# Two query tiles of one grouped head weighed by high and low values side by side, instead of two heads of one query tile

## The chip, the cores and the metric

One core of a Trainium2 chip runs the whole program. The metric is the device time of one execution in microseconds, the median of three runs. Engine names are those of the profile: PE is TensorE's matrix multiplication and PEld its loading of stationary operands, DVE is VectorE, ACT is ScalarE, POOL is GpSimd, SP issues the DMAs.

## The reference, cut to what matters

A backbone of two layers works on 512 latent tokens behind 256 context tokens, width 1024. Each layer projects the normalised input, attends in two ways (grouped heads and differential heads) beside a convolution, merges the three branches with gates, and ends in a SwiGLU feed-forward part. The grouped heads are the ones that the change touches: 8 query heads of width 64 share 2 key and value heads.

```python
def gqa_attend(q, k, v):
    s = jnp.einsum('bqkgd,btkd->bkgqt', q * ATTN_SCALE, k).astype(jnp.float32)
    p = jax.nn.softmax(s, axis=-1).astype(v.dtype)
    return jnp.einsum('bkgqt,btkd->bqkgd', p, v)
...
        o_gqa = blocked_queries(lambda qb: gqa_attend(qb, gk_all, gv_all), gq)
...
        if not last:
            oc_gqa = gqa_attend(gqc, gkc, gvc)
```

Latent queries see all 768 keys, context queries only the 256 context keys, and those are computed in layer 0 alone.

## The kernel before

Every float32 product is made of three matmuls on operands split into a high part and a low rest: high by high, high by low, low by high (`product`, lines 670 to 672).

**Heads and items.** The attention part of a layer is a walk over "heads" j = 0 to 7. Heads 0 to 3 are pairs of grouped query heads, one for each key and value head: the two members are called maps, m = 0 and m = 1, and sit in rows 0 to 63 and 64 to 127. Heads 4 to 7 are differential. An item g is one head j and one tile of 128 queries: six tiles (i = 0 to 5) in layer 0, the last two of them context queries with 256 keys (k0 = 4), and four (i = 0 to 3) in layer 1. For each item PE computes the scores of both maps (`scores`, into the PSUM tensors sco0 and sco1), DVE takes the row maximum (L1678) and ACT the exponential (L1118, M<-sco), DVE divides by the sum (`gqa_probs`, L1697 and L1698), PE transposes the probabilities into an aux bank (`turn_probs`, L874), ACT copies out the high part (`turned_hi`) and DVE the low part (`turned_lo`), and PE weighs the values with them (`weigh`). Scores run one item ahead.

**Weighing before.** The stationary operand holds the values of both maps, 64 columns each, and the moving operand the 128 queries of map 0 beside the 128 queries of map 1. Of the product only the diagonal blocks (values of map m with queries of map m) are used, and `grouped_out` copies these two out, 64x128 each. An item takes 6 x 3 matmuls of 256 columns, a context item 2 x 3.

**Slots.** Two slots per item hold projections of the next head: `slot(j, s)` runs a number of chunks, given by the tables FILL and SECOND, each chunk three matmuls (384 columns wide in layer 0, 512 in layer 1). In layer 1 a grouped head before the last has 3, 3, 2, 2, 2, 2, 1, 1 chunks in its eight slots, the first eight of them for the next query projection q, the rest for a convolution input a. When q is finished (slot 2, which is the first slot of item i = 1), ACT evacuates it in two passes and splits a weight tile (WHI, L1114); in slot 3 PE sums its squares (`head_sums`, L839), ACT makes the root, DVE rotates it (`rope`), in slot 4 DVE scales it, and in slot 5 ACT and DVE split it. `scores` of the next head waits for that split (semaphore qk).

**Order and banks.** Each engine takes its instructions in written order. Heads 0 to 2 are `late`: the item before is weighed in the middle of the next item, between its second transposition and its second slot; head 3 weighs at the item's end. PE has two acc banks (weighing and chunks) and two aux banks (transpositions and sums); an aux bank that holds turned probabilities comes free when `turned_lo` has read it on DVE.

Of the kernel before, what the change touches and what calls it, by code (L numbers as in the profile page):

```python
# [192 lines left out]
def build(nc, xT, vecs, consts, wdw, w_mod, w_in, w_gate, w_br, w_out, w_fi, w_fo, out):  # L193
    x_next = nc.dram_tensor("x_next", (P, KC, LAT), F32).ap()

    with ExitStack() as ctx:
# [14 lines left out]
        with nc.sbuf_tensor("UNDER", [P, 2 * KC * TOK], F32), nc.sbuf_tensor("SOONB", [P, 2 * KC * TOK], F32) as SOONB:  # L211
# [5 lines left out]
        STG = sb("STG", [P, STAGES, KC * P], F32)  # L217
        X = sb("X", [P, KC, TOK], F32)
# [32 lines left out]
               [v4(RB, o * TOK, 6, 256) for o in (6, 10)]]  # L251

        BR = RB[:, :].rearrange("p (s k t) -> p s k t", s=2, k=KC)
# [59 lines left out]
        late = lambda j: j < 3  # L313
        pt = lambda j, g: PTS[g % 2 if late(j) else 0]
# [311 lines left out]
        def _(pe):  # L626
# [251 lines left out]
            def weigh(name, j, g, k0, turned):  # L878
# [4 lines left out]
                for k in range(k0, 6):  # L883
                    mm = product(dst[:, 0:256], VB[:, kv, 0, k, :], VB[:, kv, 1, k, :],
                                 pt(j, g)[0][:, k, :], pt(j, g)[1][:, k, :], k == k0, k == 5)
                at[name] = c.at("acc")
                close_acc(mm, acc.index(dst))
# [6 lines left out]
            def attention(l):  # L894
# [28 lines left out]
                for g, (j, i, q, k0) in enumerate(items):  # L923
# [5 lines left out]
                    turn_probs((l, g, 0), 2 * (g % 2), k0)  # L929
                    slot(j, 2 * i)  # L930
# [6 lines left out]
                    if g and late(items[g - 1][0]):  # L937
                        k1 = items[g - 1][3]
                        weigh((l, g - 1, "o"), items[g - 1][0], g - 1, k1,
                              [at[(l, g - 1, m), p] for m in range(2) for p in range(parts(k1))])  # L940
                    if j < 4 and not late(j):
                        slot(j, 2 * i + 1)
                        weigh((l, g, "o"), j, g, k0, [at[(l, g, m), p] for m in range(2) for p in range(parts(k0))])
                        continue
# [137 lines left out]
        def _(act):  # L1082
# [83 lines left out]
            def values_hi(name, kv):  # L1166
                for i in range(2):
                    b = take_aux(at[name, i])
                    fn(VB[:, kv, 0, 3 * i:3 * i + 3, :], v4(aux[b], 0, 3, P), ACT.Copy, sem="vhi")
# [449 lines left out]
        def _(dve):  # L1619
# [143 lines left out]
            def attention(l):  # L1763
# [28 lines left out]
                for g, (j, i, q, k0) in enumerate(items):  # L1792
# [6 lines left out]
                    if j < 4:  # L1799
                        slot(j + 1, 2 * i)  # L1800
# [486 lines left out]
```

## Time and profile before

| | |
|---|---|
| median of 3 runs | 2417.32 us (2414.1 to 2419.98) |
| span of the profiled execution | 2417.6 us |
| PE busy, of the span | 2347.1 us, 97% |
| PEld busy | 2117.3 us, 88% |
| DVE busy | 1379.6 us, 57% |
| ACT busy | 1027.8 us, 43% |
| grouped heads of layer 0 (scores of head 0 to those of head 4) | about 88 to 267 us |
| grouped heads of layer 1 | about 1484 to 1647 us |

No time of the profiled execution is given beside its span. Busy time of PE counts matmuls that overlap each other, so the distance from one start to the next tells what a matmul costs.

### The profile page before, as it was taken

How to read it: one execution, taken by the hardware profiler on the slowest of the kernel's cores; microseconds unless marked ns; L12 is line 12 of the kernel's file. 1: busy time of each engine (PE TensorE's matmuls, PEld its weight loads, DVE VectorE, ACT ScalarE, POOL GpSimd, SP SyncE). 2: the span in 40 equal slices, each digit the busy share in tenths (PEclk: the TensorE clock that was granted, in tenths of full speed). 3: DMA queues.
4: the chain of work that ended last, by engine and by line, in shares of the span. 5: the costliest groups of instructions: out<-in, count | busy, mean ns of one | idle time of the engine just before them, and what ended most of it. 6: DMA issues, size and time to landing. Idle time of an engine off the chain costs nothing.

```text
span 2417.6 us, 33460 instructions
## 1 busy us (share of the span) xinstructions
PE 2347.1 (97%) x13144; PEld 2117.3 (88%) x13144; DVE 1379.6 (57%) x2097; ACT 1027.8 (43%) x2039; POOL 698.9 (29%) x513
## 2 busy tenths in 40 slices
PE   7999999999999989999999999999999998999999
PEld 3888999999999989999999997777878887888887
DVE  5666777689967735553343347667888944211111
ACT  4666676642253242212212237666764354422222
POOL 2211112100034424343343333112220154444443
PEclk9999999999999989999999999999999999999999
DMA  6100111022124413433443421011113323333333
GB/s 255 45 19 27 40 40 36 31 92 88 61 83 137 164 57 114 132 109 116 129 134 98 127 96 53 27 36 45 50 35 92 100 89 125 92 100 96 97 96 96
DMA packets 134667, 208.99 MB, mean 86 GB/s; under 512 B 12528, under 2 KB 66032, under 8 KB 134384
## 3 DMA queue, kind: packets, MB, share of 16 engines
q1 hardware_dynamic: 134512, 206.86, 27.1%
q8 instruction: 105, 1.72, 0.3%
q14 instruction: 50, 0.41, 0.1%
HBM read 202.62 MB, written 4.19 MB: 86 GB/s over the span
## 4 chain that ended last, share of the span: by engine, by line
PE 77%; DVE 14%; ACT 6%; issue 3%; DMA 1%; SPq 0%; DVEq 0%; ACTq 0%
PE acc L670 20%; PE acc L672 20%; PE acc L671 20%; DVE X L1758 4%; PE aux L670 3%; PE aux L671 3%; PE aux L672 3%; DVE RB L1635 2%; PE sco L861 2%; PE aux L874 2%; ACT M L1118 2%; DVE M L1635 1%; DVE NM L1678 1%; ACT WHI L1114 1%; DVE WLO L1635 1%
## 5 line engine op out<-in xcount | busy, mean ns | idle before, releaser
L586 POOL TENSOR_TENSOR WLO<-STG,WHI 128x512 fp32r<-128x512 f32 (+2 forms) x500 | 692.0, 1406 | 1700.9 <-ACT WHI L1114 1536.2
L670 PE MATMUL acc<-H,WHI 128*128 128x384 f32 (+2 forms) x1976 | 712.8, 361 | 14.5 <-DVE H L1911 8.7
L671 PE MATMUL acc<-H,WHI 128*128 128x384 f32 (+2 forms) x1976 | 696.9, 353 | 0.0
L672 PE MATMUL acc<-H,WLO 128*128 128x384 f32 (+2 forms) x1976 | 696.7, 353 | 0.0
L1114 ACT ACTIVATE WHI<-STG 128x512 fp32r<-128x512 f32 (+2 forms) x616 | 330.2, 584 | 402.1 <-PE acc L672 365.4
L670 PEld LDWEIGHTS acc<-H,WHI 128*128 128x128 f32 x1976 | 375.4, 190 | 44.4 <-issue 13.0
L672 PEld LDWEIGHTS acc<-H,WLO 128*128 128x128 f32 x1976 | 375.0, 190 | 25.4
L671 PEld LDWEIGHTS acc<-H,WHI 128*128 128x128 f32 x1976 | 375.8, 190 | 24.0
L670 PE MATMUL acc<-RB,WHI 128*128 128x384 f32 (+1 forms) x816 | 288.5, 354 | 3.2 <-DVE RB L1635 1.5
L1635 DVE TENSOR_TENSOR T<-G,acc 128x384 f32<-128x384 f32 (+1 forms) x101 | 60.2, 596 | 405.4 <-PE acc L672 290.1
L672 PE MATMUL acc<-RB,WLO 128*128 128x384 f32 (+1 forms) x816 | 287.6, 352 | 0.0
L671 PE MATMUL acc<-RB,WHI 128*128 128x384 f32 (+1 forms) x816 | 287.6, 352 | 0.0
L1758 DVE SCALAR_TENSOR_TENSOR X<-U,WDW,X 128x783 f32<-128x783 f32 (+1 forms) x248 | 219.3, 935 | 4.9 <-ACT X L1118 3.3
L1976 DVE SCALAR_TENSOR_TENSOR X<-acc,MOD,X 128x384 f32<-128x384 f32 (+3 forms) x124 | 65.0, 547 | 242.9 <-PE acc L672 242.8
L670 PE MATMUL aux<-H,WHI 128*128 128x384 f32 (+1 forms) x552 | 197.6, 358 | 1.0 <-DVE WLO L1635 1.0
L671 PE MATMUL aux<-H,WHI 128*128 128x384 f32 (+1 forms) x552 | 195.8, 355 | 0.0
L672 PE MATMUL aux<-H,WLO 128*128 128x384 f32 (+1 forms) x552 | 195.6, 354 | 0.0
L1678 DVE TENSOR_REDUCE NM<-sco 128x1 f32<-128x768 f32 (+1 forms) x160 | 134.8, 844 | 66.0 <-PE sco L861 65.9
L670 PEld LDWEIGHTS acc<-RB,WHI 128*128 128x128 f32 x816 | 153.2, 188 | 15.3 <-DVE RB L1635 1.8
L671 PEld LDWEIGHTS acc<-RB,WHI 128*128 128x128 f32 x816 | 153.2, 188 | 10.7
L672 PEld LDWEIGHTS acc<-RB,WLO 128*128 128x128 f32 x816 | 153.2, 188 | 10.6
L1118 ACT ACTIVATE M<-sco,NM 128x768 f32<-128x768 f32 (+1 forms) x160 | 131.1, 820 | 61.4 <-DVE NM L1678 61.2
(148 smaller groups left out, 2934.3 us busy)
## 6 DMA issues: line engine op xcount, KB each, us to landing
STG<-in_w_fi SPq DMA_DIRECT2D x176, 256.0 KB, 2.7
M<-in_w_mod SPq DMA_DIRECT2D x56, 512.0 KB, 4.9
STG<-in_w_in SPq DMA_DIRECT2D x104, 256.0 KB, 2.7
STG<-in_w_gate SPq DMA_DIRECT2D x96, 256.0 KB, 2.7
STG<-in_w_fo SPq DMA_DIRECT2D x64, 256.0 KB, 2.7
STG<-in_w_br SPq DMA_DIRECT2D x96, 128.0 KB, 2.1
FIRST<-in_w_mod SPq DMA_DIRECT2D x8, 1024.0 KB, 20.2
SOONB<-in_w_mod SPq DMA_DIRECT2D x16, 512.0 KB, 4.1
```

Of the source, the lines that this page charges most:

```text
L586: nc.gpsimd.tensor_tensor(WLO[:, s, a:a + w], STG[:, g, a:a + w], WHI[:, s, a:a + w].bitcast(F32), ALU.subtract).then_inc(S("w_split"), 1)
L670: nc.tensor.matmul(dst, lh, rh, start=first, stop=False)
L671: nc.tensor.matmul(dst, lh, rl, start=False, stop=False)
L672: return nc.tensor.matmul(dst, ll, rh, start=False, stop=last)
L861: mm = nc.tensor.matmul(sco[m][:, o:o + w], QB[h, j % 2, x, q:q + P], KB[h, kv, y, a:a + w], start=n == 0, stop=n == 2)
L874: t = nc.tensor.transpose(dst[:, n * P:(n + 1) * P], PR[:, slot, (k - k0) * P:(k - k0 + 1) * P], IDENT)
L1114: nc.scalar.activation(WHI[:, s, a:a + w], STG[:, g, a:a + w], ACT.Copy).then_inc(S("w_hi"), 1)
L1118: ins = nc.scalar.activation(dst, src, f, **kw)
L1635: return nc.vector.tensor_tensor(dst, a, b, op)
L1678: nc.vector.tensor_reduce(NM[:, slot:slot + 1], sco[m][:, 0:n], AX_X, ALU.max, negate=True).then_inc(S(f"max{m}"), 1)
L1758: nc.vector.scalar_tensor_tensor(o, like(l, U[:, ch * UW + t:ch * UW + t + w0]), WDW[:, l, ch, t:t + 1], o, ALU.mult, ALU.add).then_inc(S( ...
L1976: nc.vector.scalar_tensor_tensor(X[:, j, s:s + m], src[:, s - a:s - a + m], MOD[:, l, part, j, st:st + 1], X[:, j, s:s + m], ALU.mult, ALU ...
```

## The change

Weighing is done once for two query tiles (items i = 0 and 1, 2 and 3, 4 and 5) and one map at a time. The stationary operand is now the high values of one map beside its low values, 64 columns each (`VGM`, two matmuls a key tile: one with the high probabilities moving, one with the low), and the moving operand has 256 columns, the queries of both tiles. Rows of the high values and of the low values come out apart, so ACT copies one half (`grouped_lo`) and DVE adds the other to it (`grouped_sum`), which also frees the acc bank. Map 0 is weighed at the end of the odd item, map 1 in the next item, after its first transposition and ahead of its first slot. Turned probabilities of map 1 lie in a new tensor XP, in the upper half of the room of X. The exception of head 3 is gone, so that DVE turns the low part of map 1 behind `gqa_probs` for all grouped heads. Two bias copies of the convolution in layer 1 move from head 3 to head 4.

```diff
+        with nc.sbuf_tensor("UNDERX", [P, 4 * TOK], F32), nc.sbuf_tensor("XP", [P, 2 * 6 * 256], F32R) as XP:
+            pass
...
+        VG = RB[:, 8 * TOK:10 * TOK].rearrange("p (k b d) -> p k b d", k=6, b=4)
+        VGH, VGL = VG[:, :, 0:4:3, :], VG[:, :, 1:3, :]
+        VGM = RB[:, 8 * TOK:10 * TOK].rearrange("p (k m c) -> p k m c", k=6, m=2)
...
-        late = lambda j: j < 3
-        pt = lambda j, g: PTS[g % 2 if late(j) else 0]
+        grouped_pair = lambda item: item[0] < 4 and item[1] % 2
...
+            def weigh_map(l, g, k0, m):
+                wait_free("aux", *(at[(l, e, m), p] for e in (g - 1, g) for p in range(2 if k0 == 0 else 1)))
+                dst = open_acc()
+                for k in range(k0, 6):
+                    for s in range(2):
+                        mm = nc.tensor.matmul(dst[:, 0:256], VGM[:, k, m, :], PTS[m][s][:, k, :],
+                                              start=(k == k0 and s == 0), stop=(k == 5 and s == 1))
+                at[l, g, "o", m] = c.at("acc")
+                close_acc(mm, acc.index(dst))
...
                     turn_probs((l, g, 0), 2 * (g % 2), k0)
+                    if g and grouped_pair(items[g - 1]):
+                        weigh_map(l, g - 1, items[g - 1][3], 1)
                     slot(j, 2 * i)
...
-                    if g and late(items[g - 1][0]):
-                        k1 = items[g - 1][3]
-                        weigh((l, g - 1, "o"), items[g - 1][0], g - 1, k1,
-                              [at[(l, g - 1, m), p] for m in range(2) for p in range(parts(k1))])
...
                     slot(j, 2 * i + 1)
+                    if grouped_pair((j, i)):
+                        weigh_map(l, g, k0, 0)
...
-            def grouped_out(l, g, j, q):
-                b = take(at[l, g, "o"])
-                for m in range(2):
-                    rows = slice(m * HEAD, m * HEAD + HEAD)
-                    fn(X[rows, j, q:q + P], acc[b][rows, m * P:(m + 1) * P], ACT.Copy,
-                       sem=f"acc_free{b}" if m else "oraw")
+            def grouped_lo(l, g, j, q, m):
+                b = take(at[l, g, "o", m])
+                rows, lows = (slice(n * HEAD, n * HEAD + HEAD) for n in (m, 1 - m))
+                fn(X[rows, j, q - P:q + P], acc[b][lows, 0:256], ACT.Copy, sem="glo")
...
                     if after:
                         exp(0, g + 1, after[3])
                         exp(1, g + 1, after[3])
+                    if g and grouped_pair(items[g - 1]):
+                        grouped_lo(l, g - 1, items[g - 1][0], items[g - 1][2], 1)
                     slot(j + 1, 2 * i)
...
+            def grouped_sum(l, g, j, q, m):
+                b, _ = banks["acc"][at[l, g, "o", m]]
+                c.step("glo")
+                dve.wait_ge(S("glo"), c.at("glo"))
+                rows = slice(m * HEAD, m * HEAD + HEAD)
+                o = X[rows, j, q - P:q + P]
+                tt(o, o, acc[b][rows, 0:256], ALU.add).then_inc(S(f"acc_free{b}"), 1)
...
                         maximum(1, g + 1, after[3])
+                    if g and grouped_pair(items[g - 1]):
+                        grouped_sum(l, g - 1, items[g - 1][0], items[g - 1][2], 1)
                     if j < 4:
                         slot(j + 1, 2 * i)
-                    if j < 4 and not late(j):
-                        turned_lo((l, g, 1), pt(j, g), P, k0)
                     if after and after[0] < 4:
                         gqa_probs(g + 1, after[3])
...
                     slot(j + 1, 2 * i + 1)
+                    if grouped_pair((j, i)):
+                        grouped_sum(l, g, j, q, 0)
```

Where the instructions stand is read from the program's order. On PE, at the end of item i = 1 of a grouped head in layer 1, before: the last matmuls of the item before being weighed (acc<-RB), the two chunks of slot 3 (acc<-H), the sums of squares for the next query projection (aux<-M,K), and the next scores.

```order
L671 MATMUL acc<-RB 128x256
L672 MATMUL acc<-RB 128x256
L670 MATMUL acc<-H,WHI 128x512
L671 MATMUL acc<-H,WHI 128x512
L672 MATMUL acc<-H,WLO 128x512
L670 MATMUL acc<-H,WHI 128x512
L671 MATMUL acc<-H,WHI 128x512
L672 MATMUL acc<-H,WLO 128x512
L839 MATMUL aux<-M,K 128x256 x2
L861 MATMUL sco<-RB 128x512 x6
```

The same place of PE after the change, from the second transposition of the item (aux<-K,M) on; L903 is `weigh_map`.

```order
L881 MATMUL aux<-K,M 128x128 x6
L677 MATMUL acc<-H,WHI 128x512
L678 MATMUL acc<-H,WHI 128x512
L679 MATMUL acc<-H,WLO 128x512
L677 MATMUL acc<-H,WHI 128x512
L678 MATMUL acc<-H,WHI 128x512
L679 MATMUL acc<-H,WLO 128x512
L846 MATMUL aux<-M,K 128x256 x2
L903 MATMUL acc<-RB 128x256 x12
L868 MATMUL sco<-RB 128x512 x6
```

Between the second transposition and the sums of squares there stand two chunks now and no weighing; map 0 is weighed behind the sums.

On DVE, item i = 2 of such a head before: maximum of map 0, low part of the turned map 0, maximum of map 1, scaling of q (M<-M,R), division of both maps, low part of the turned map 1, low part of q.

```order
L1678 TENSOR_REDUCE NM<-sco 128x1
L1635 TENSOR_TENSOR RB<-aux,RB 128x3x128 x2
L1678 TENSOR_REDUCE NM<-sco 128x1
L1635 TENSOR_TENSOR M<-M,R 128x512
L1697 RECIPROCAL RL<-L 128x1
L1698 TENSOR_SCALAR M<-M,RL 128x768
L1697 RECIPROCAL RL<-L 128x1
L1698 TENSOR_SCALAR M<-M,RL 128x768
L1635 TENSOR_TENSOR RB<-aux,RB 128x3x128 x2
L1635 TENSOR_TENSOR RB<-M,RB 128x512
```

The same item of DVE after the change, with the sum of map 0 of the pair before ahead of it.

```order
L1652 TENSOR_TENSOR X<-X,acc 64x256
L1698 TENSOR_REDUCE NM<-sco 128x1
L1652 TENSOR_TENSOR RB<-aux,RB 128x3x128 x2
L1698 TENSOR_REDUCE NM<-sco 128x1
L1652 TENSOR_TENSOR X<-X,acc 64x256
L1652 TENSOR_TENSOR M<-M,R 128x512
L1726 RECIPROCAL RL<-L 128x1
L1727 TENSOR_SCALAR M<-M,RL 128x768
L1726 RECIPROCAL RL<-L 128x1
L1727 TENSOR_SCALAR M<-M,RL 128x768
L1652 TENSOR_TENSOR XP<-aux,XP 128x3x128 x2
L1652 TENSOR_TENSOR RB<-M,RB 128x512
```

The sum of map 1 has come in between the second maximum and everything that the item does afterwards.

## Rows read from the trace of the kernel before

**Rows 1.** The page: busy time of each engine, share of the span.
```profile
PE 2347.1 (97%) x13144; PEld 2117.3 (88%) x13144; DVE 1379.6 (57%) x2097; ACT 1027.8 (43%) x2039; POOL 698.9 (29%) x513
```

**Rows 2.** Windows: head 1 of layer 1, head 2 of layer 0; columns as in the first line.
```profile
core 0: us, PE busy (x) PEld busy (x) DVE busy (x) ACT busy (x) POOL busy (x), PEclk, DMA share, GB/s
1528.20:1562.30 34.10, 32.49 (x223) 26.78 (x222) 24.74 (x47) 22.24 (x51) 5.06 (x4) 1.00 0.10 32
177.90:221.00 43.10, 42.32 (x301) 37.52 (x300) 30.16 (x64) 27.90 (x72) 5.06 (x4) 1.00 0.08 25
```

**Rows 3.** Timeline, PE: second matmul of a weighing of 18, and the first behind it.
```profile
212.16 0.28 PE L671 MATMUL acc<-RB 128*128 128x256 f32 x1
...
214.19 0.34 PE L670 MATMUL acc<-H,WHI 128*128 128x384 f32 x1
```

**Rows 4.** Timeline, PE, layer 1: scores that open four items of one head, and the next head's.
```profile
1553.27 1.32 PE L861 MATMUL sco<-RB 64*128 64x512 f32 x12
...
1562.29 1.32 PE L861 MATMUL sco<-RB 64*128 64x512 f32 x12
...
1565.64 0.82 PE L874 MATMUL aux<-K,M 128*128 128x128 f32 x6
1570.88 1.10 PE L839 MATMUL aux<-M,K 128*128 128x256 f32 x4 [0.45 <-DVE RB L1635]
1571.91 1.32 PE L861 MATMUL sco<-RB 64*128 64x512 f32 x12
...
1580.60 1.31 PE L861 MATMUL sco<-RB 64*128 64x512 f32 x12 [0.75 <-DVE RB L1635]
...
1587.35 1.32 PE L861 MATMUL sco<-RB 64*128 64x512 f32 x12
```

**Rows 5.** Timeline, ACT and DVE, item i = 1 of that head.
```profile
1568.61 1.16 ACT L1114 ACTIVATE WHI<-STG 128x512 fp32r<-128x512 f32 x2
1569.65 0.87 ACT L1118 ACTIVATE RB<-aux 128x384 fp32r<-128x384 f32 x2
...
1570.17 1.02 DVE L1635 TENSOR_TENSOR RB<-aux,RB 128x384 fp32r<-128x384 f32 x2 [1.76 <-ACT RB L1118]
```

**Rows 6.** Timeline, ACT and DVE, item i = 2 of that head.
```profile
1576.60 0.90 ACT L1118 ACTIVATE M<-sco,NM 128x768 f32<-128x768 f32 x1 [0.80 <-DVE NM L1678]
1577.40 0.19 ACT L1118 ACTIVATION_READ_ACCUMULATOR M<-sco,NM 128x1 f32 x1
...
1575.62 0.95 DVE L1678 TENSOR_REDUCE NM<-sco 128x1 f32<-128x768 f32 x1
...
1578.54 1.01 DVE L1635 TENSOR_TENSOR RB<-aux,RB 128x384 fp32r<-128x384 f32 x2
1579.76 0.69 DVE L1635 TENSOR_TENSOR RB<-M,RB 128x512 fp32r<-128x512 f32 x1 [0.21 <-ACT RB L1118]
```

**Rows 7.** Groups by line and shape: the nearest to the new operations.
```profile
L1118 ACT ACTIVATE X<-acc 64x128 f32<-64x128 f32 x80 | 21.7, 271 | 19.6 <-PE acc L672 17.6
L1118 ACT ACTIVATE X<-acc 128x256 f32<-128x256 f32 x20 | 7.6, 382 | 14.3 <-PE acc L672 14.3
L1635 DVE TENSOR_TENSOR RB<-aux,RB 128x256 fp32r<-128x256 f32 x24 | 10.0, 418 | 4.4 <-ACT RB L1118 4.2
```

**Rows 8.** Timeline, PEld, layer 0, item i = 1: the chunk behind the weighing.
```profile
190.76 0.19 PEld L670 LDWEIGHTS acc<-H,WHI 128*128 128x128 f32 x1 [0.35 <-ACT M L1118]
```

**Rows 9.** Windows around idle stretches of PE; timeline of the waits that end them.
```profile
2054.00:2056.00 2.00, 2.00 (x7) 1.52 (x6) 2.00 (x4) 1.97 (x3) 0.00 (x0) 0.50 0.00 0
2056.00:2058.00 2.00, 2.00 (x9) 1.59 (x8) 2.00 (x4) 1.94 (x5) 0.00 (x0) 0.79 0.00 0
...
2053.35 0.69 PE L670 MATMUL acc<-H,WHI 128*128 128x512 f32 x1 [3.40 <-DVE H L1911]
...
1634.00:1636.00 2.00, 1.45 (x14) 1.30 (x15) 0.54 (x2) 0.38 (x1) 0.00 (x0) 1.00 0.47 153
...
1634.55 1.32 PE L861 MATMUL sco<-RB 64*128 64x512 f32 x12 [1.61 <-DVE RB L1635]
```

More of the change, by code:

```diff
@@ L250, in build @@
         PTS = [[PT[:, s] for s in range(2)],
-               [v4(RB, o * TOK, 6, 256) for o in (6, 10)]]
+               [v4(XP, s * 6 * 256, 6, 256) for s in range(2)]]
+        VG = RB[:, 8 * TOK:10 * TOK].rearrange("p (k b d) -> p k b d", k=6, b=4)
+        VGH, VGL = VG[:, :, 0:4:3, :], VG[:, :, 1:3, :]
+        VGM = RB[:, 8 * TOK:10 * TOK].rearrange("p (k m c) -> p k m c", k=6, m=2)
+        pairs = lambda t: t[:, 0:3 * P].rearrange("p (k m d) -> p k m d", k=3, m=2)
         BR = RB[:, :].rearrange("p (s k t) -> p s k t", s=2, k=KC)
@@ L1168, in values_hi @@
                     b = take_aux(at[name, i])
-                    fn(VB[:, kv, 0, 3 * i:3 * i + 3, :], v4(aux[b], 0, 3, P), ACT.Copy, sem="vhi")
+                    if name[1] == 0:
+                        fn(VGH[:, 3 * i:3 * i + 3], pairs(aux[b]), ACT.Copy, sem="vhi")
+                    else:
+                        fn(VB[:, kv, 0, 3 * i:3 * i + 3, :], v4(aux[b], 0, 3, P), ACT.Copy, sem="vhi")
             def evac_conv_a(l, ch, use, a, w):
@@ L1290, in attention @@
                         exp(1, g + 1, after[3])
+                    if g and grouped_pair(items[g - 1]):
+                        grouped_lo(l, g - 1, items[g - 1][0], items[g - 1][2], 1)
                     slot(j + 1, 2 * i)
                     if j < 4:
-                        turned_hi((l, g, 1), pt(j, g), P, k0)
-                    if g and late(items[g - 1][0]):
-                        grouped_out(l, g - 1, items[g - 1][0], items[g - 1][2])
-                    if j < 4:
+                        turned_hi((l, g, 1), PTS[1], P * (i % 2), k0)
                         slot(j + 1, 2 * i + 1)
-                        if not late(j):
-                            grouped_out(l, g, j, q)
+                        if i % 2:
+                            grouped_lo(l, g, j, q, 0)
                     elif i % 2:
@@ L1307, in attention @@
                         slot(j + 1, 2 * i + 1)
-                    if l and j == 3:
+                    if l and j == (3 if i < 2 else 4):
                         conv_bias(l, i)
@@ L1795, in attention @@
                         maximum(0, g + 1, after[3])
-                    turned_lo((l, g, 0), pt(j, g), 0 if j < 4 else P * (i % 2), k0)
+                    turned_lo((l, g, 0), PTS[0], P * (i % 2), k0)
                     if after:
                         maximum(1, g + 1, after[3])
+                    if g and grouped_pair(items[g - 1]):
+                        grouped_sum(l, g - 1, items[g - 1][0], items[g - 1][2], 1)
                     if j < 4:
                         slot(j + 1, 2 * i)
-                    if j < 4 and not late(j):
-                        turned_lo((l, g, 1), pt(j, g), P, k0)
                     if after and after[0] < 4:
```

18 lines of the change are left out of this document (9 added, 9 removed).

## The prediction

> **What bounds the kernel now.** I read the page first. PE is busy for 97% of the span, DVE for 57% and ACT for 43% [rows 1], so over the whole kernel a matmul less is time less. The windows of single heads then show where the change works. Head 2 of layer 0 keeps PE busy for 42.3 of 43.1 us, head 1 of layer 1 for 32.5 of 34.1 us [rows 2]. Those shares flatter PE, because matmuls overlap: the 223 matmuls in the second window include 72 of weighing that each stand in the row with 0.28 us but follow one another at 0.12 us [rows 3]. The timeline gives the item lengths of a grouped head in layer 1, from one opening score to the next: 9.02, 9.62, 8.69 and 6.75 us, 34.08 together [rows 4]. In i = 1 PE sits waiting for DVE before the sums of squares, and in i = 2 it waits 0.75 us for DVE to hand over the next head's q [rows 4]. So these heads are near a balance: PE has the most work, but the round from scores through maximum, exponential, division, transposition and back is almost as long. What the change is worth must be read there.
>
> **What it removes.** A pair of items took 2 x 18 matmuls of 256 columns and takes 2 x 12: 12 fewer, or 4 fewer for the context pair. Layer 0 has four heads with two long pairs and one context pair, 4 x 28 = 112; layer 1 has four heads with two long pairs, 4 x 24 = 96. That is 208 matmuls. Their shape stays, and one costs (214.19 - 212.16) / 17 = 0.119 us [rows 3]. The sum is 24.8 us, 1.0% of the time. This is the ceiling of the gain.
>
> The Trainium skill ("TensorE: Matmul & The Clock Gate", section "Wait — 56ns, not 53.3ns?") puts the distance of warm matmuls at the columns over 2.4 GHz plus about 2.5 ns. By that rule a matmul of 256 columns costs 0.109 us, and the ceiling would be 22.7 us instead of 24.8; the row is 9% above it, and the sum goes by the row.
>
> **What it adds.** On ACT 80 copies of 64x128 (0.271 us) become 40 of 64x256, which lie between 0.271 and 0.382, the row of 128x256 [rows 7]. I take 0.38, since the columns are the same. ACT gains some 6 us of work that it has to spare. On DVE 40 additions of 64x256 out of PSUM are new. The nearest row has 256 columns and a PSUM operand, 0.418 us [rows 7]; I take 0.4, with 0.271 and 0.55 as ends (a copy of half the width, and a third above the row). That is 16 us of DVE work. By themselves neither would matter. What matters is where they stand, because each waits, and everything behind it on its engine waits too.
>
> **The sum of map 1 in an even item.** It stands on DVE right behind the second maximum. ACT's copy for it stands behind both exponentials. The second exponential starts when the second maximum is done and takes 1.1 us with its accumulator read [rows 6]. So from the end of that maximum DVE waits 1.1 + 0.4 us, adds for 0.4, and only then divides. Before, the division of map 0 ran during that exponential. In i = 2 the low part of map 1 began 1578.54 - 1576.57 = 1.97 us behind the end of the maximum, 0.6 of scaling and both divisions (about 1.4 to 1.5) included [rows 6]; now it can begin at 1.5 + 0.4 + 0.6 + 1.5 = 4.0. Without the scaling the second division had to wait for the exponential, and the difference is some 1.5 us. By so much every even item of a grouped head hands over its low parts later.
>
> **Item i = 1 in layer 1.** The second transposition starts 3.35 us into the item and the sums of squares 8.59 us into it [rows 4]. The latter need aux banks that are freed only when DVE has read the turned map 1. DVE's read waits for ACT, which first does q's evacuation and the weight split [rows 5]. None of this changes. What did fill PE meanwhile was the weighing, 2.2 us, and it is gone from there: two chunks (1.4 us) remain. Map 0 is weighed behind the sums, 1.45 us with nothing to cover. The item becomes 8.6 + 1.1 + 1.45 + some 0.4 of lateness that DVE brings along from i = 0 = 11.6 us instead of 9.62, with PE idle for about 3.1 us in it.
>
> **Item i = 2 in layer 1.** It must deliver q before the next head's scores. Before, the second maximum began 3.71 us into the item and the split of q ended 8.54 us into it, 0.15 us before the scores [rows 4, 6]. The rotation made that maximum some 0.3 late, which ends now, because the item starts later. The chain becomes 4.25 (second maximum done) + 1.5 + 0.4 + 0.6 (scaling) + 1.5 (divisions) + 1.0 (low part of map 1) + 0.7 (low part of q) + 0.15 = 10.1 us instead of 8.69. PE is through with its own work at 6.9 and idles for 3.2 us.
>
> **Items 3 and 0 in layer 1** carry 0.72 us less PE work each and have no such wait: 6.0 and 8.2 instead of 6.75 and 9.02. Head sum: 8.2 + 11.6 + 10.1 + 6.0 = 35.9, **1.8 us longer** than 34.08. That holds for heads 1 and 2. Head 0 has no pair ahead of its item 0 and gets +2.0. Head 3 has 8 to 16 chunks an item, and its divisions now run while DVE waits for ACT: -4.1. The last weighing falls into head 4: +1.4. **Layer 1: +2 x 1.8 + 2.0 - 4.1 + 1.4 = +2.9 us.**
>
> **Layer 0.** q is finished a pair earlier relative to its use, so there is no wait for q. But in i = 1 map 0 opens the acc bank that q's first half has just left. Already now PE waits 0.35 us for that evacuation [rows 8]; with DVE 1.8 us late after i = 0 (the sum of map 1, and map 0's copy behind a weight split), and the evacuation behind the exponentials, it comes about 1 us too late for the weighing. By the same step of each engine the items come to 6.2, 9.7, 6.6, 10.0, 5.4 and 5.1 us, 43.0 against the 43.1 of before [rows 2]. Heads 1 and 2 gain 0.1 each, head 0, with fewer chunks and q ready earlier, 1.5. Head 3 is full of chunks and gets all its 28 matmuls back, 3.3. **Layer 0: -5.0 us.**
>
> **The clock.** PE's idle stretches of 3.1 and 3.2 us are new. Rows of before show what such stretches do: behind 3.40 us of idling the granted clock was 0.50, the lower of its two levels (1.2 instead of 2.4 GHz), and some 3.4 us went by at it; behind 1.61 us it stayed at 1.00 [rows 9]. Mine are nearer to the longer one. At the low level 3.4 us of work lose half, 1.7 us. Six such stretches stand in layer 1 (two in each of heads 0 to 2). I take half of them as caught: +5 us; none and all, 0 and +10, are the ends.
>
> **Sum.** 2.9 - 5.0 + 5 = +2.9 us against the span of 2417.6. That execution lies 0.3 above the median of 2417.32, so the forecast is **2420 us**. A measurement of this kernel can tell about 0.2%, 4.8 us, from no change, so this reads as no change.
>
> **The rivals.**
> (a) The matmuls come through. PE is busy for 97% of the span and everywhere in the chain. If DVE's and ACT's waits were absorbed by slack as before, the time is 2417.3 - 24.8 = 2392. Against it speaks the order of DVE: the sum stands ahead of the division. Chance 0.08.
> (b) Half comes through: the waits are as I say in i = 1 and 2 of layer 1, but layer 0 pays less (its DVE is busy for 30 of 43 us [rows 2]) and the clock stays up. Layer 0 then gives 4 x 3.3 = 13 instead of 5, and layer 1 costs 0 to 3: 2404 to 2407. Chance 0.22.
> (c) Slower, by the clock: each of the six stretches is caught, and two of layer 0 in i = 1 and i = 3 as well. 2417.3 - 2.1 + 8 x 1.7 = 2429; it decides from about four caught stretches on (2422). The Trainium skill, same page, section "Loop structure matters more than you think", warns of waits between matmuls that send PE to the lower clock, with 8 us as its case; no row here is that long, and 3.40 us sufficed [rows 9]. Chance 0.24.
> (d) Slower, by a longer wait: the additions take 0.55 us and ACT's copies queue behind a further split, 0.3 us for each of the 20 pairs, +6: 2426. Chance 0.10.
> My own case has the rest, 0.36, and spans 2412 to 2422.
>
> **How the numbers follow.** Faster: (a) and (b), 0.30. Within 0.2%: 0.36. Slower: (c) and (d), 0.34. The range leaves out (a) below and the worst of (c) above: 2403 to 2430.
>
> **What would show it.** PE's count falls by 208. In layer 1, i = 1 of heads 0 to 2 should be about 11.6 us long with an idle stretch of about 3 us before the sums of squares (releaser DVE); i = 2 about 10.1 us with as much idling before the scores (releaser DVE, the split of q). On DVE the addition behind the second maximum should stand idle for about 1.5 us, put down to ACT's copy into X. Heads 3 of both layers should be shorter by 3 to 4 us. The granted clock of those windows tells the part of the clock: 1.00 throughout takes 5 us off my sum. I am wrong if grouped heads 1 and 2 of layer 0 come out at 40 us (rival b), or if idle stretches stay under 2 us.

## The result, and the profile after

The changed kernel takes **2432.95 us** (median of 6 runs, 2425.74 to 2436.73), the kernel before 2418.92 us (median of 6, 2414.1 to 2420.76). The ratio is 1.0053, with a 95% interval of 1.0041 to 1.0064. The change makes the kernel slower by half a per cent, 14 us by the medians. The forecast was 2420 us, 2403 to 2430, no change: it was wrong.

The profiled execution took 2431.45 us, with a span of 2429.7 us against 2417.6. First the page's line of busy times. It answers to [rows 1].

```profile
PE 2335.7 (96%) x12936; PEld 2106.6 (87%) x12936; DVE 1394.0 (57%) x2137; ACT 1024.7 (42%) x1999; POOL 697.0 (29%) x513
```

The change did what it says: PE has 208 matmuls fewer, DVE 40 additions more, ACT 40 copies fewer. And PE is busy for only 11.4 us less, where 24.8 us were taken away. That hints that some of the matmuls that are left are slower; the windows and rows below show it.

The windows show where. The first two are head 1 of layer 1 and head 2 of layer 0, which answer to [rows 2] (columns as there; the window of layer 1 in [rows 2] starts one item into head 1, and from opening score to opening score that head took 34.05 us). The others are stretches of layer 1's heads 0, 1 and 2.

```profile
1523.23:1561.47 38.24, 32.11 (x197) 26.94 (x196) 26.52 (x51) 21.72 (x48) 5.03 (x4) 0.91 0.11 28
177.66:220.29 42.63, 39.11 (x274) 34.46 (x274) 32.44 (x70) 27.87 (x67) 5.06 (x4) 1.00 0.09 26
...
1500.00:1510.00 10.00, 7.91 (x49) 7.09 (x50) 6.64 (x12) 5.45 (x12) 2.50 (x2) 0.83 0.18 55
1550.00:1560.00 10.00, 6.88 (x36) 5.45 (x35) 7.11 (x15) 3.40 (x8) 0.00 (x0) 0.83 0.00 1
1590.00:1600.00 10.00, 7.46 (x35) 6.54 (x36) 6.58 (x14) 3.55 (x9) 0.00 (x0) 0.66 0.01 2
```

The head of layer 0 went from 43.10 to 42.63 us, with PE idle for 3.5 us of it instead of 0.8. The head of layer 1 went from 34.10 to 38.24 us. Its granted clock was 0.91, where it was 1.00. Over 1485 to 1602 us the window has 0.90 after, and 1.00 before.

The timeline of PE in head 2 of layer 1 answers to [rows 4].

```profile
1561.47 1.32 PE L868 MATMUL sco<-RB 64*128 64x512 f32 x12
...
1569.78 1.32 PE L868 MATMUL sco<-RB 64*128 64x512 f32 x12
...
1578.36 2.04 PE L846 MATMUL aux<-M,K 128*128 128x256 f32 x4 [3.02 <-DVE XP L1652]
1579.85 2.66 PE L903 MATMUL acc<-RB 128*128 128x256 f32 x12
1582.44 1.32 PE L868 MATMUL sco<-RB 64*128 64x512 f32 x12
...
1592.54 2.29 PE L868 MATMUL sco<-RB 64*128 64x512 f32 x12 [3.10 <-DVE RB L1652]
...
1600.95 1.32 PE L868 MATMUL sco<-RB 64*128 64x512 f32 x12
```

The two waits that were forecast are there, 3.02 and 3.10 us. Behind each the same work is slower: twelve score matmuls take 2.29 us instead of 1.32, four matmuls of sums 2.04 instead of 1.10 us [rows 4]. The items are 8.31, 12.66, 10.10 and 8.41 us long. The forecast had 8.2, 11.6, 10.1 and 6.0. The excess, 1.1 and 2.4 us, stands exactly where the clock is low.

DVE and ACT in item i = 2 of head 1 show the first half of the cause. Both maxima, then the addition (X<-X,acc), the scaling, two divisions, the low part of map 1 (XP) and the low part of q (RB), for which the scores wait.

```profile
1547.35 0.95 DVE L1698 TENSOR_REDUCE NM<-sco 128x1 f32<-128x768 f32 x1
1548.33 0.90 ACT L1133 ACTIVATE M<-sco,NM 128x768 f32<-128x768 f32 x1 [0.69 <-DVE NM L1698]
1549.13 0.19 ACT L1133 ACTIVATION_READ_ACCUMULATOR M<-sco,NM 128x1 f32 x1
1549.35 0.38 ACT L1133 ACTIVATE X<-acc 64x256 f32<-64x256 f32 x1
...
1549.76 0.42 DVE L1652 TENSOR_TENSOR X<-X,acc 64x256 f32<-64x256 f32 x1 [1.46 <-ACT X L1133]
1550.21 0.69 DVE L1652 TENSOR_TENSOR M<-M,R 128x512 f32<-128x512 f32 x1
...
1552.39 1.02 DVE L1652 TENSOR_TENSOR XP<-aux,XP 128x384 fp32r<-128x384 f32 x2
1553.33 0.68 DVE L1652 TENSOR_TENSOR RB<-M,RB 128x512 fp32r<-128x512 f32 x1
1554.16 1.42 PE L868 MATMUL sco<-RB 64*128 64x512 f32 x6 [3.10 <-DVE RB L1652]
```

DVE stands for 1.46 us (forecast 1.5) because ACT's copy sits behind the second exponential. The copy costs 0.38 us and the addition 0.42 us, as priced. PE gets q at 1554.1.

There is one wait that the forecast does not have: the first chunks of head 4's first item in layer 0. The timeline of ACT, DVE and PE there:

```profile
278.39 1.28 ACT L1133 ACT_TABLE_LOAD   x1
279.69 0.84 ACT L1133 ACTIVATE M<-M 128x768 f32<-128x768 f32 x1
280.55 1.28 ACT L1139 ACT_TABLE_LOAD   x1
...
281.84 1.15 ACT L1129 ACTIVATE WHI<-STG 128x512 fp32r<-128x512 f32 x2
...
283.01 0.38 ACT L1133 ACTIVATE X<-acc 64x256 f32<-64x256 f32 x1
...
283.43 0.41 DVE L1652 TENSOR_TENSOR X<-X,acc 64x256 f32<-64x256 f32 x1 [1.84 <-ACT X L1133]
...
283.89 0.44 PE L677 MATMUL acc<-H,WHI 128*128 128x384 f32 x1 [3.04 <-DVE X L1652]
```

And the window around the end of that wait (columns as in [rows 2]):

```profile
283.00:288.00 5.00, 4.11 (x15) 4.11 (x16) 3.12 (x6) 3.61 (x8) 2.06 (x2) 0.67 0.35 107
```

Head 3's last weighing of map 0 was ready, but the copy that frees its acc bank is behind two table loads, a sigmoid and a weight split on ACT. PE waits 3.04 us for the bank, and the granted clock of the window is 0.67: the item takes 13.69 us, and 8.50 before (from one opening score to the next, 282.71 to 291.21 before, 278.25 to 291.94 after).

**Where the 12.1 us of span lie**, from the opening scores of both traces: the start of the first layer's attention is 1.4 us later, ahead of anything that the change touches. Layer 0's attention takes 389.9 instead of 390.9 us, -1.0: head 0 -1.2, heads 1 and 2 -0.5 each, head 3 -3.7, head 4's first item +5.2, the rest -0.3. The stretch between the two attentions is 1.1 us shorter. Layer 1's attention up to its last item takes 318.0 instead of 306.8, +11.1: heads 0 to 2 +14.3 (+4.7, +4.2, +5.4), head 3 -6.5, head 4 on +3.3. The last item takes 14.21 instead of 12.65, +1.6, and what follows 0.1 more. Two of these shares are one more stretch at the low clock, and neither is shown to be the change's: ahead of layer 0's attention the clock is 0.50 from 21.90 to 28.70 us, before only from 22.50 to 25.90, and in the last item it falls behind a wait of 2.7 us that the kernel before has too (last section).

### The profile page after: what moved, and what is told of

The parts are those of the page before. It is cut to its first block, busy times and chain, and to the rows that moved or that the text cites. A ratio compares the mean times of both kernels' runs of the same rounds, so it can differ in the third digit from the quotient of the medians.

```text
span 2429.7 us, 33044 instructions
## 1 busy us (share of the span) xinstructions
PE 2335.7 (96%) x12936; PEld 2106.6 (87%) x12936; DVE 1394.0 (57%) x2137; ACT 1024.7 (42%) x1999; POOL 697.0 (29%) x513
## 4 chain that ended last, share of the span: by engine, by line
PE 78%; DVE 13%; ACT 6%; issue 3%; DMA 1%; SPq 0%; DVEq 0%; ACTq 0%
PE acc L677 19%; PE acc L679 19%; PE acc L678 19%; PE aux L677 4%; PE aux L678 4%; PE aux L679 4%; DVE X L1787 3%; ACT M L1133 2%; DVE RB L1652 2%; PE sco L868 2%; DVE NM L1698 2%; PE aux L881 2%; DVE M L1652 2%; PE acc L903 1%; PE aux L846 1%
```

## The experiments

The theory after this profile: the waits are the forecast's, the clock falls behind each of the six in layer 1, and a bank held over the border of heads 3 and 4 costs another 5 us. One rival is that the idling alone explains the loss, without the clock; another that the new additions cost as much wherever they stand. Eleven kernels were run. Ratios are to the kernel before, on the same chip in the same minutes. The groups e1 to e4, e5 to e8 and e9 to e11 ran on three chips, so kernels of different groups are compared by their ratios.

**e1: the clock alone.** The changed kernel with work for PE in its two waits of a head in layer 1: 20 matmuls of 256 columns into a corner of the scores' PSUM that nobody reads.

```
+                def keep_busy():
+                    pe.wait_ge(S("exp"), c.at("sc"))
+                    for _ in range(20):
+                        nc.tensor.matmul(sco[0][:, 768:1024], H[:, 0, 0, 0:P], H[:, 0, 0, 0:256], start=True, stop=True)
...
+                    if l and j < 3 and s in (3, 5):
+                        keep_busy()
```

> The changed kernel with 20 extra matmuls of 256 columns (2.4 us of work into unused columns of sco0, nothing reads them) in each of the six idle stretches of heads 0 to 2 of layer 1, ahead of the sums of squares in item 1 and ahead of the next scores in item 2. Theory 1 (PE's idle stretches of 3 us lower the granted clock, and each costs about 1.7 us of slow work): the granted clock stays at 1.00 in those heads, the item lengths fall from about 12.4, 10.3 and 7.5 to about 11.5, 10.1 and 6.2, in all 8 to 10 us below the changed kernel, 1.001 to 1.002 of the kernel before. Rival (the clock is only a bystander, the waits for DVE are everything): no gain, or up to 2 us more, 1.005 to 1.006.

Measured: 2420.15 us (12 runs), 1.0008 (0.9998 to 1.0019). PE's rows of items i = 1 and 2 of head 2:

```profile
1574.58 2.58 PE L925 MATMUL sco<-H 128*128 128x256 f32 x20
...
1577.77 1.10 PE L846 MATMUL aux<-M,K 128*128 128x256 f32 x4 [0.61 <-DVE XP L1659]
...
1587.05 2.56 PE L925 MATMUL sco<-H 128*128 128x256 f32 x20
...
1590.31 1.33 PE L868 MATMUL sco<-RB 64*128 64x512 f32 x12 [0.70 <-DVE RB L1659]
```

And a window in each of the two items:

```profile
1572.00:1582.00 10.00, 9.39 (x69) 8.11 (x68) 7.35 (x16) 6.67 (x14) 2.52 (x2) 1.00 0.18 53
1590.00:1597.00 7.00, 6.45 (x48) 5.43 (x50) 5.04 (x11) 4.15 (x10) 0.00 (x0) 1.00 0.01 2
```

120 matmuls more, and 11 us less by the ratios. PE's next real instruction comes when it came before, since DVE decides that, but the clock is 1.00 and the items are 8.29, 11.03, 10.10 and 6.06 us. The forecast had 8.2, 11.6, 10.1 and 6.0, so all but i = 1 (0.6 us too long) are met. With the clock taken out, heads 0 to 2 are 5.0 us longer than before (107.95 from 1488.42 to 1596.37, against 102.97), where the forecast had 5.6. So of the 14.3 us in these heads some 9.3 are the clock's. The rival without the clock falls.

**e2: the addition of map 1 behind the division.** One move on DVE, everywhere:

```
                     if after:
                         maximum(1, g + 1, after[3])
-                    if g and grouped_pair(items[g - 1]):
-                        grouped_sum(l, g - 1, items[g - 1][0], items[g - 1][2], 1)
                     if j < 4:
                         slot(j + 1, 2 * i)
                     if after and after[0] < 4:
                         gqa_probs(g + 1, after[3])
                     elif after:
                         diff_probs(l, g + 1, after[3])
+                    if g and grouped_pair(items[g - 1]):
+                        grouped_sum(l, g - 1, items[g - 1][0], items[g - 1][2], 1)
```

> The changed kernel with one line moved: DVE adds map 1's halves behind the division of the next probabilities instead of ahead of it. Theory 1 (the addition waits for ACT's copy behind both exponentials and holds up everything behind it): item 2 in layer 1 becomes 1.5 us shorter in each of three heads, its idle stretch shrinks to about 1.7 us and the clock is not lowered behind it; with that 9 to 12 us below the changed kernel, 1.000 to 1.002 of the kernel before. Rival (DVE has slack there and the place of the addition does not matter): within 2 us of the changed kernel, 1.005.

Measured: 2427.52 us (7 runs), 1.0036 (1.0023 to 1.0049), between the two theories. In layer 1 the wait ahead of the scores in i = 2 fell from 3.10 to 1.55 us, by the 1.5 us of the forecast's term, and heads 1 and 2 became 35.4 and 33.9 us long (38.2 and 39.5 in the changed kernel). But DVE and PE of item i = 4 in layer 0's head 1 show that it is paid elsewhere:

```profile
168.38 0.96 DVE L1652 TENSOR_TENSOR RB<-M,RB 128x768 fp32r<-128x768 f32 x1 [1.90 <-ACT RB L1133]
...
170.29 0.42 DVE L1652 TENSOR_TENSOR X<-X,acc 64x256 f32<-64x256 f32 x1
...
170.77 0.67 PE L677 MATMUL acc<-H,WHI 128*128 128x384 f32 x1 [2.48 <-DVE X L1652]
```

In that item q's split and the divisions stand ahead of the addition, and with it the acc bank stays taken: 9.65 us instead of 5.52. Head 2 pays 8.28 instead of 5.51 in the same place: PE waits 2.48 us in both, but only in head 1 does the clock fall behind it. Layer 1's head 3 takes 15.24 instead of 12.41 in i = 2. In the profiled executions heads 0 to 2 of layer 1 give 11.0 us, layer 0's attention takes back 6.4 and layer 1's head 3 2.9. The same move is a gain in one item and a loss in another.

**e3: map 0 weighed, copied and added ahead of the odd item's second slot.** On PE, ACT and DVE the same exchange of two steps; PE's part:

```
-                    slot(j, 2 * i + 1)
                     if grouped_pair((j, i)):
                         weigh_map(l, g, k0, 0)
+                    slot(j, 2 * i + 1)
```

> The changed kernel with map 0 weighed ahead of the odd item's second slot instead of behind it, and ACT's copy and DVE's addition moved likewise. Theory 1 (the weighing is the cover for the wait before the sums of squares, and at the end of head 3 the copy sits behind a sigmoid with its table loads while the acc bank is held): item 1 in layer 1 falls from 12.4 to about 9.7, the 3 us wait and the lowered clock at the start of head 4 in layer 0 vanish (5 us), and the whole is 14 to 17 us below the changed kernel, 0.998 to 1.000 of the kernel before. Rival (the wait only moves to the bank of q or to the next scores): 0 to 4 us below the changed kernel.

Measured: 2424.69 us (10 runs), 1.0021 (1.001 to 1.0033). The weighing now fills the wait in i = 1 (9.6 us instead of 12.4; a wait of 0.44 us is left), but the wait in i = 2 grew from 3.10 to 3.82 us, because DVE is just as late and PE is sooner there. Much of what one item gave, the next took. The other half of the theory missed: at the start of head 4 in layer 0 PE still waits 2.75 us for a bank, and the item takes 13.27 us (13.69).

**e4: the border of heads 3 and 4, map 0 only.** In head 3's last item, ACT's copy and DVE's addition of map 0 stand ahead of the last slot's work:

```
+                        last_of_3 = j == 3 and i == len(qtiles(l)) - 1
+                        if last_of_3:
+                            grouped_lo(l, g, j, q, 0)
                         slot(j + 1, 2 * i + 1)
-                        if i % 2:
+                        if i % 2 and not last_of_3:
                             grouped_lo(l, g, j, q, 0)
```

> The changed kernel with ACT's copy and DVE's addition of map 0 ahead of the last slot's work in the last item of head 3 only; PE's order is untouched. Theory 1 (the first chunk of head 4 waits 3 us for the acc bank because ACT's copy stands behind the sigmoid, its two table loads and a weight split): item 0 of head 4 in layer 0 falls from 9.8 and 13.7 over two items to 9.5 and 8.5 or so, about 5 us below the changed kernel, and 1 to 1.5 us more in layer 1. Rival (the chunk waits for the weights or for something else): no gain, 1.005.

Measured: 2431.57 us (6 runs), 1.0052 (1.0036 to 1.0067): nothing gained. The trace shows why. Head 4's first item is 13.77 us long:

```profile
273.69 0.38 ACT L1133 ACTIVATE X<-acc 64x256 f32<-64x256 f32 x1 [1.80 <-PE acc L903]
...
282.97 0.42 DVE L1655 TENSOR_TENSOR X<-X,acc 64x256 f32<-64x256 f32 x1 [1.46 <-ACT X L1133]
...
283.54 0.66 PE L677 MATMUL acc<-H,WHI 128*128 128x384 f32 x1 [3.18 <-DVE X L1655]
```

Map 0's copy is now in time (273.69), and PE runs on to its ninth chunk, where it waits 3.18 us for map 1's bank, whose copy stands behind the same table loads, a split and two exponentials. My account of this border was too narrow.

**e6: the border, both maps.** e4, and at the start of head 4 map 1's copy ahead of the exponentials (below) and its addition ahead of the second maximum:

```
                     turned_hi((l, g, 0), PTS[0], P * (i % 2), k0)
+                    if j == 4 and i == 0:
+                        grouped_lo(l, g - 1, items[g - 1][0], items[g - 1][2], 1)
                     if after:
                         exp(0, g + 1, after[3])
                         exp(1, g + 1, after[3])
-                    if g and grouped_pair(items[g - 1]):
+                    if g and grouped_pair(items[g - 1]) and j < 4:
                         grouped_lo(l, g - 1, items[g - 1][0], items[g - 1][2], 1)
```

> The run before last of this place moved only map 0's copy, and the wait came back at the ninth chunk, for map 1's bank. Here map 1's copy and addition at the start of head 4 also stand ahead of the exponentials. Theory 1 (both acc banks are held because ACT is 4.6 us behind there: table load, sigmoid, table load, weight split): the item of 13.7 us in layer 0 falls to about 8.6, and the clock behind it stays up: 5 us below the changed kernel, 1.003. Rival (ACT is too late by itself and the order there does not matter): the item stays above 11 us, 1.005.

Measured: 2426.11 us (11 runs), 1.0028 (1.0019 to 1.0037), 0.25% or 6 us under the changed kernel. Head 4's first item takes 9.91 us in layer 0 and 11.83 in layer 1 (13.18 before this move). Both stay some 1.4 us above the kernel before (8.50 and 10.38). In layer 1 that is the price of map 1's twelve matmuls (1.45 us), which are now weighed in this item. In layer 0, where 8.6 was expected, it is four such matmuls (0.5 us) and a wait of 0.88 us for map 1's bank that is left at the ninth chunk. The rest of what the held banks cost, 3.8 us in layer 0 and 1.4 in layer 1, is gone: the second half of the loss. Moving map 1's part alone was not run.

**e5 and e7: the moves together.** e5 is e2 and e3; e7 adds map 1's part of e6 to it (map 0's is in e3 already).

> Both moves at once: map 0 weighed ahead of the odd item's second slot, and DVE's addition of map 1 behind the division. Theory 1 (two separate waits: the cover gone in item 1 and the addition ahead of the division in item 2): layer 1's items come to about 8.3, 9.6, 9.2 and 6.0, 33.1 a head against 34.1 before and 38.2 to 39.5 in the changed kernel, with idle stretches under 2.5 us and few lowered clocks there; 12 us or more below the changed kernel, 0.997 to 1.000 of the kernel before, with head 4 of layer 0 still losing 4 to 5 us. Rival (one chain of DVE bounds these heads, whatever the order): a head stays at 36 us or more, 1.002.

> Both moves inside the heads and both at the boundary to head 4. Theory 1 (the gains add up since the waits are separate): 5 us below the run with both moves, 0.994 to 0.998 of the kernel before. Rival (the gains overlap, or the waits move to the next head's scores): 0.998 to 1.000.

Measured: e5 2431.26 us (5 runs), 1.0056 (1.0043 to 1.0068); e7 2422.78 us (11 runs), 1.0018 (1.0009 to 1.0027). Both missed. Layer 1's heads 1 and 2 did come out at 34.3 us, but the additions behind the division held the bank in more places than e2 had shown: layer 0's attention took 398.5 us in e5 and 396.0 in e7, against 387.4 in e6. In e7 items i = 4 and 5 of heads 1 and 2 took 8.6, 6.1, 9.1 and 5.6 us (e6: 5.5, 4.9, 5.5, 4.9), head 3's second last 14.2 (9.8), and layer 1's head 3 3.9 us more.

**e8: no additions at all.** ACT's copy frees the bank, and the output holds only one of the two halves of each grouped head's weighing.

```
-                fn(X[rows, j, q - P:q + P], acc[b][lows, 0:256], ACT.Copy, sem="glo")
+                fn(X[rows, j, q - P:q + P], acc[b][lows, 0:256], ACT.Copy, sem=f"acc_free{b}")
...
             def grouped_sum(l, g, j, q, m):
+                return
```

> The changed kernel without DVE's 40 additions: ACT's copy frees the acc bank, and the high half of the product is left out, so the grouped heads' output holds the low part only. PE's and ACT's order is that of the changed kernel. Theory 1 (of the loss some 1.9 us per item 2 hang on the additions' wait, the rest on the cover that item 1 lost): item 1 of layer 1 stays at 11.0 to 12.5 with its 3 us wait, item 2 falls from 10.2 to 8.3 with no lowered clock behind it, layer 0's item 1 falls from 9.4 to about 8.2: 12 to 15 us below the changed kernel, 0.999. Rival (DVE's work as such, 16 us, is the bound): more than 20 us below it, 0.996 or less.

Measured: 2415.48 us (11 runs), 0.9986 (0.9978 to 0.9995). The 40 additions, 17 us of DVE's time, cost 16 us of the kernel's, by what waits behind them: in the profiled execution heads 0 to 2 of layer 1 are 11.1 us shorter, with three stretches at the low clock instead of seven, and layer 0's attention 4.8. But not all: the wait ahead of the sums in i = 1 stays at 3.03 us and still brings the low clock, and at the border PE still waits 2.60 us, now for ACT's copy alone. The wait in i = 2 falls to 0.99 us:

```profile
1568.64 2.05 PE L846 MATMUL aux<-M,K 128*128 128x256 f32 x4 [3.03 <-DVE XP L1652]
...
1580.50 1.31 PE L868 MATMUL sco<-RB 64*128 64x512 f32 x12 [0.99 <-DVE RB L1652]
...
277.02 0.44 PE L677 MATMUL acc<-H,WHI 128*128 128x384 f32 x1 [2.60 <-ACT X L1133]
```

**e9: the addition behind the division in one item only.** e7, with the addition of map 1 back behind the second maximum, but for i = 2 of heads 0 to 2.

```
+                    if g and grouped_pair(items[g - 1]) and j < 4 and not (i == 2 and j < 3):
+                        grouped_sum(l, g - 1, items[g - 1][0], items[g - 1][2], 1)
                     if j < 4:
                         slot(j + 1, 2 * i)
...
-                    if g and grouped_pair(items[g - 1]) and j < 4:
+                    if g and grouped_pair(items[g - 1]) and i == 2 and j < 3:
                         grouped_sum(l, g - 1, items[g - 1][0], items[g - 1][2], 1)
```

> The changed kernel with map 0's product, copy and addition ahead of the odd tile's second slot, map 1's copy and addition at the start of head 4 ahead of the exponentials and the second maximum, and map 1's addition behind the next tile's division in one place only: in tile 2 of heads 0 to 2. Theory 1 (what undid the two combined runs was the addition behind the division in the other places: in layer 0 it waits there until 170.29 behind a split of 0.96 us and two divisions, and PE stands 2.7 us for the bank; at head 3 it stands behind a longer division): against the combined run with the boundary (span 2421.1) tile items of layer 0's heads 1 and 2 fall from 8.6, 6.1, 9.1, 5.6 to 5.5, 4.9, 5.5, 4.9 (-8.5 us), layer 0's item at head 3's end from 14.2 to 9.5 (-4.7), and head 3 of layer 1 loses 3.8 less: -17 us, a span near 2404, a ratio of 0.9935 to 0.996, under the kernel before. Theory 2 (the additions cost what they cost wherever they stand, and what one place gains another gives back): the combined run's 1.002 stays.

**e10** puts e1's 20 matmuls into the one wait of e9 that is left in these heads (i = 2). **e11** is e6 with e1's matmuls.

> The kernel of the last run with 20 matrix products of 256 columns, whose result nobody reads, at the one wait that is left in layer 1's heads 0 to 2: ahead of the next tile's scores in tile 2, where PE stands 2.28 us. Theory 1 (a wait of 2.3 us at this place still lets the clock fall, 1.7 us for each of three): the clock is 1.00 in layer 1's first three heads, and the time falls by 4 to 5 us more, a ratio 0.002 lower than the last run's. Theory 2 (2.3 us is too short to matter, or the extra products take as much from the engine as the clock gives): no difference, or up to 1 us slower.

> The changed kernel with both of its losses taken away and nothing else: map 0's copy and addition ahead of the last slot of head 3, map 1's at the start of head 4, and 20 matrix products of 256 columns without a reader at each of the two waits of a head in layer 1. Theory 1 (the two losses are independent, 5.5 us of clock and waits in layer 1 and 6 us at head 4): they add, and with the 0.9978 +- 0.001 that follows from 1.0053 - 0.0045 - 0.0024 it is under the kernel before by 3 to 7 us, a ratio of 0.997 to 0.999. Theory 2 (the change itself is slower even so, through its 72 more additions and copies a layer): 1.000 or more.

Measured: e9 **2408.48 us** (6 runs), 0.9963 (0.9951 to 0.9976); e10 2407.4 us (5 runs), 0.9955 (0.9943 to 0.9968); e11 2415.67 us (11 runs), 0.999 (0.9981 to 1.0). (e11's expectation speaks of 72 additions and copies a layer; there are 40 in both layers together.) The windows of 117 us from about the start of layer 1's head 0 on, in e9, e10 and e11 (they reach into head 3):

```profile
1485.00:1602.00 117.00, 105.21 (x677) 86.89 (x674) 87.40 (x170) 75.03 (x161) 17.72 (x14) 0.96 0.10 32
```

```profile
1485.00:1602.00 117.00, 111.18 (x742) 91.85 (x740) 90.54 (x176) 76.59 (x165) 17.76 (x14) 1.00 0.11 33
```

```profile
1485.00:1602.00 117.00, 111.68 (x773) 96.05 (x772) 84.89 (x164) 72.57 (x156) 17.70 (x14) 1.00 0.10 30
```

e9 is faster than the kernel before by 0.24 to 0.49%, and than the changed one by 0.9%. The additions behind the division were what undid e5 and e7: layer 0's attention takes 383.4 us, 12.5 less than in e7 (13.2 expected). It ends just above its expected range. In layer 1's head 3 it gained 3.1 of the 3.8 us; where the rest is missing stays open. In the profiled execution each of the three waits of 2.28 us in i = 2 still brings the low clock, but e7 had the same three, so they do not explain the shortfall. In e10 the clock stays at 1.00 there and heads 0 to 2 are 3.0 us shorter in the profiled execution (1479.87 to 1584.25 in e9, 1479.11 to 1580.47 in e10), but the medians differ by 1 us only and the intervals overlap: that this pays in time is not shown, and the 4 to 5 us expected did not come. One reason may be that e9's profiled execution is among its two slowest: their mean clock is 0.985, and that of the other four 0.988 to 0.990, as high as in e10 (0.988 to 0.990). e11 is what two independent losses give: 1.0053 less 0.0045 (e1) and 0.0025 (e6) is 0.9983, inside its interval (the 0.9978 in its expectation is a slip). With both gone, the change is at or a little below the time before, 0.999.

## Why the prediction was wrong

**What held.** The counts (208 matmuls, 40 additions, 40 copies), the prices (0.38 and 0.42 us against 0.38 and 0.4), the 1.5 us that DVE stands ahead of the addition (1.46), both waits of a head in layer 1 (3.0 and 3.1 us against 3.1 and 3.2) and, as e1 showed, the item lengths of heads 1 and 2 in layer 1 (i = 1 was 0.6 us shorter than forecast). In layer 0 the items of head 1 came as 6.36, 9.32, 6.80, 9.68, 5.52 and 4.94, 42.6 us against a forecast of 43.0. Rivals (a) and (b), a gain that comes through, were rightly put aside: 24.8 us of matmuls are gone, and in the heads' windows idle time and slower matmuls have taken their place.

**The step that failed first: the clock.** "I take half of them as caught: +5 us." All six were, one of them twice: in the trace seven stretches of some 3.4 us stand at the low level in heads 0 to 2. They cost 9.3 us by the comparison with e1. That is a mis-sized term, and it was the one with the widest bounds, 0 to 10. The prediction says itself that its stretches are nearer to the row of 3.40 us than to that of 1.61, and then takes half without a reason. In the profiled executions of e5, e7 and e9 even the waits of 2.28 us brought the low clock, nine times of nine. Rival (c) had all six caught and two more in layer 0, and came out at 2429. It was nearest, partly by luck: in i = 1 and 3 of layer 0's heads 1 and 2 the clock stayed at 1.00 (waits of 1.32 and 1.39 us), and the stretch that did come there was at the border of heads 3 and 4, which it did not have. The Trainium skill ("TensorE: Matmul & The Clock Gate", section "Loop structure matters more than you think") warns of matmul loops with waits between them and has 8 us as its case. By direction the trace agrees; by length it goes much further down, as the 2.28 us show, and the last section has one of 1.67.

**The step that was missing: the border of heads 3 and 4.** "Layer 0: -5.0 us" came out as -1.0, because the sum ended with head 3 ("gets all its 28 matmuls back, 3.3", measured 3.7) and took the last weighing's price for head 4 from layer 1 only. In layer 0 it costs 5.2 us, of which e6 leaves 1.4, the four matmuls of the weighing (0.5) and a wait of 0.88 us; the other 3.8 are the longer wait for the bank and the clock behind it. The last item of head 3 is where the rotation of the weighing leaves two banks taken, while ACT has table loads, a sigmoid, a split and two exponentials queued. I had listed what stands ahead of map 1's copy in an even item, but not in this one, where the queue is another. e4 gained nothing in layer 0 by map 0's copy alone, e6 took the wait away with both. With it go layer 1's head 4, +3.3 instead of +1.4, and the other way head 3, -6.5 instead of -4.1, for which no run looks for the cause.

**The sum again**: forecast +2.9; the clock +4.3 more, heads 0 to 2 of layer 1 otherwise -0.6, layer 0 +4.0, head 3 of layer 1 -2.4, head 4 +1.9, and +2.0 elsewhere (the start +1.4, between the attentions -1.1, layer 1's last item +1.6, behind it +0.1) make +12.1, the difference of the spans. The last is no cost of the change that I can show: the stretch between the attentions, whose work no kernel here changes, took from 999.9 to 1007.2 us in the thirteen profiled executions. The medians are 14 us apart, two more than the spans; that part stays open.

**The share of the additions.** "By themselves neither would matter. What matters is where they stand" is half borne out: 17 us of DVE work cost 16 us in e8, nearly their own length and no small thing. But e9, with all 40 of them in, is by the ratios 22 us under the changed kernel, by the place of map 1's addition in i = 2, of map 0's weighing and of the copies at the border together.

## What to carry to other kernels

A wait that appears on TensorE is priced twice, by its own length and by half of what runs behind it at the low clock (9.3 us for seven stretches here, 1.3 each, and 1.7 where PE has work throughout); where the nearest caught stretch is about as long, take all of them as caught, and put filler work or a reordering beside it in the plan. When an accumulator's evacuation becomes two steps on two engines, write down for every place where it occurs what is queued ahead of each step: the ordinary place may be fine while the one at a change of phase, with table loads and splits, holds the bank. The best position of such a step is not one for all places: ahead of the division it delayed the critical data, behind it it held a bank.

## What the runs showed of the hardware

The low clock does not follow from a wait's length alone. Waits of 3.0 us in item i = 1 were followed by it in heads 0 and 1 of e2, but not in head 2, where the item is 11.04 us long instead of head 1's 12.55. The two timeline rows of e2, of heads 1 and 2:

```profile
1546.60 2.04 PE L846 MATMUL aux<-M,K 128*128 128x256 f32 x4 [3.03 <-DVE XP L1652]
...
1582.05 1.10 PE L846 MATMUL aux<-M,K 128*128 128x256 f32 x4 [3.02 <-DVE XP L1652]
```

And the windows of e2 around these two waits:

```profile
1540.00:1550.00 10.00, 6.97 (x32) 5.73 (x31) 7.34 (x15) 7.13 (x15) 2.49 (x2) 0.83 0.19 51
...
1575.00:1585.00 10.00, 6.97 (x44) 5.76 (x44) 7.73 (x15) 7.67 (x16) 2.50 (x2) 1.00 0.15 51
```

The same holds for one wait in two executions. Near the end of layer 1's attention PE waits 2.7 us for a split on DVE, before the change and after it. The row of after:

```profile
1809.30 0.36 PE L677 MATMUL acc<-RB 128*128 128x256 f32 x1 [2.75 <-DVE RB L1652]
```

The kernel before has the same wait with 2.72 us, and its last item is 12.65 us long; after, it is 14.21 us. This wait, 2.72 to 2.75 us in all thirteen profiled executions, was followed by the low clock in nine; it went by without in those of the kernel before, e2, e6 and e11.

A much shorter wait can be caught, and a longer one spared. In head 3 of layer 1 e9 waits 1.67 us, and the clock falls behind it:

```profile
1607.27 1.07 PE L881 MATMUL aux<-K,M 128*128 128x128 f32 x6 [1.67 <-ACT R L1133]
...
1609.00:1612.00 3.00, 3.00 (x12) 2.66 (x11) 2.04 (x5) 0.76 (x2) 0.00 (x0) 0.50 0.46 148
```

e5 and e7 show the same, the other ten executions have this wait (1.66 or 1.67 us) and keep the clock at 1.00. Between the two attentions e7 waits 3.38 us and keeps it, where the kernel before, with the same 3.38 us, lost it:

```profile
687.62 1.58 PE L761 MATMUL acc<-U,K 128*128 128x392 f32 x4 [3.38 <-DVE U L1654]
...
687.00:692.00 5.00, 4.38 (x22) 3.82 (x23) 3.89 (x8) 1.99 (x3) 0.00 (x0) 1.00 0.00 0
```

That executions of one kernel differ by how many such waits are caught fits their times: the six runs of the changed kernel lie 11 us apart, and their mean clock goes with their time, 0.987 at 2425.74 us and 0.982 at 2436.73 us. A forecast of such a kernel should give the number of waits that can be caught, and a range that spans their cost.
